# A layer of three mixers and product-key experts in one launch: a query projection from rows that are not yet normalised, another order of the mixers' outputs, and rotary tables made at the start

## The reference, cut to what matters

```python
h = rms_norm(x, norm1_g)                          # x: 256 tokens x 1024
ua, qb, kb, vb, qc, kc, vc, gc = split(h @ w_in)
ya = rms_unit(s5_mixer(ua, ...))                  # state space, gelu, y * sigmoid(y @ w_glu), 256 wide
yb = rms_unit(moba_mixer(qb, kb, vb, ...))        # causal attention here: 8 heads of 64, 512 wide
yc = retention_mixer(qc, kc, vc, gc, ...)         # 4 heads of 64, a norm per head, silu gate
x = x + (concat([ya, yb, yc]) * mix_out_g) @ w_out
h2 = rms_norm(x, norm2_g)                         # rms_norm(x, g) = x * rsqrt(mean(x*x) + eps) * g
q = (h2 @ w_q).reshape(t, 8, 2, 64)
sc = einsum('thcd,hcnd->thcn', q, sub_keys)       # scores, then top 16 of 128, twice, then of the pairs
out = x + sum_k gate_k * gelu(h2 . u_emb[e_k]) * v_emb[e_k]   # 16384 experts, 16 per head and token
```

## Time and profile before

| | us |
|---|---|
| median of 3 runs | 925.8 |
| lowest, highest | 925.78, 928.47 |
| the profiled execution | 925.64 |
| its span | 923.9 |
| TensorE busy | 910.5 |
| VectorE, ScalarE, POOL busy | 688.7, 539.8, 425.2 |

### The profile page before, as it was taken

How to read it: one execution, slowest core, us unless ns; L and a number is a source line. 1 busy time by engine, 2 the same in 40 slices (tenths; PEclk the granted TensorE clock), 3 DMA queues, 4 the chain that set the end, 5 groups by cost and what they waited for, 6 DMA issues and landing times.

```text
span 923.9 us, 20024 instructions
## 1 busy us (share of the span) xinstructions
PE 910.5 (99%) x5900; PEld 823.4 (89%) x5900; DVE 688.7 (75%) x1533; ACT 539.8 (58%) x1061; POOL 425.2 (46%) x340
## 2 busy tenths in 40 slices
PE   8999999999999999999999999999999999999998
PEld 7777879999999999999999999888888888888886
DVE  7989421079998027888888886888888888888886
ACT  7658655555555555555555555665656565656563
POOL 5764286788888877777777775000000000000000
PEclk9999999999999999999999999999999999999999
DMA  9644050456666666566555656777677777777773
GB/s 333 228 159 157 27 205 1 160 187 226 228 229 229 226 209 206 193 199 198 189 198 192 196 190 215 252 242 245 232 245 241 242 236 244 244 243 234 243 244 125
DMA packets 67756, 191.53 MB, mean 207 GB/s; under 512 B 6673, under 2 KB 8593, under 8 KB 67729
## 3 DMA queue, kind: packets, MB, share of 16 engines
q1 hardware_dynamic: 67728, 191.19, 61.5%
HBM read 173.86 MB, written 17.30 MB: 207 GB/s over the span
## 4 chain that ended last, share of the span: by engine, by line
PE 75%; POOL 11%; issue 7%; ACT 3%; DVE 2%; DMA 0%; POOLq 0%; SPq 0%; DVEq 0%
PE ps L429 23%; PE ps L431 22%; PE ps L430 22%; POOL w_lo L1600 11%; PE ps L717 3%; PE ps L414 1%; DVE ps L774 1%; ACT w_hi L1277 1%; DVE routing L774 1%; ACT routing L1343 0%; POOL w_lo L1585 0%; DMA xs<-in_x 0%; PE ps L603 0%; PE ps L406 0%; ACT L1265 0%
## 5 line engine op out<-in xcount | busy, mean ns | idle before, releaser
L1495 ACT ACTIVATE w_hi<-raw 128x512 fp32r<-128x512 f32 x512 | 308.3, 628 | 137.0 <-PE ps L431 134.8
L1600 POOL TENSOR_TENSOR w_lo<-raw,w_hi 128x512 fp32r<-128x512 f32 x256 | 327.1, 1299 | 81.1 <-ACT w_hi L1495 80.3
L429 PE MATMUL ps<-h_hi,w_hi 128*128 128x256 f32 x1088 | 308.6, 284 | 1.8 <-POOL w_lo L1600 1.1
L431 PE MATMUL ps<-h_hi,w_lo 128*128 128x256 f32 x1088 | 307.9, 283 | 0.0
L430 PE MATMUL ps<-h_lo,w_hi 128*128 128x256 f32 x1088 | 307.8, 283 | 0.0
L774 DVE TENSOR_TENSOR w_lo<-raw,w_hi 128x512 fp32r<-128x512 f32 x256 | 177.4, 693 | 56.1 <-ACT w_hi L1495 41.2
L429 PEld LDWEIGHTS ps<-h_hi,w_hi 128*128 128x128 f32 x1088 | 208.7, 192 | 2.7 <-POOL w_lo L1600 1.3
L430 PEld LDWEIGHTS ps<-h_lo,w_hi 128*128 128x128 f32 x1088 | 208.8, 192 | 0.0
L431 PEld LDWEIGHTS ps<-h_hi,w_lo 128*128 128x128 f32 x1088 | 208.8, 192 | 0.0
L429 PE MATMUL ps<-w_hi,hot_gate 128*128 128x512 f32 x512 | 199.2, 389 | 0.0
L430 PE MATMUL ps<-w_lo,hot_gate 128*128 128x512 f32 x512 | 199.2, 389 | 0.0
(11 more groups left out here) (207 smaller groups left out, 841.7 us busy)
## 6 DMA issues: line engine op xcount, KB each, us to landing
raw<-in_u_t SPq DMA_DIRECT2D x128, 512.0 KB, 3.4
raw<-in_v SPq DMA_DIRECT2D x128, 512.0 KB, 3.3
act_spill<-acts SPq DMA_DIRECT2D x62, 256.0 KB, 2.1
acts<-act_spill SPq DMA_DIRECT2D x62, 256.0 KB, 3.4
routing<-in_w_in SPq DMA_DIRECT2D x4, 2048.0 KB, 12.4
routing<-in_w_out SPq DMA_DIRECT2D x2, 2048.0 KB, 8.4
routing<-in_w_q SPq DMA_DIRECT2D x2, 2048.0 KB, 7.9
routing<-in_w_in SPq DMA_DIRECT2D x2, 1024.0 KB, 9.7
```

What stands on the lines that cost most here:

```text
L429: pe.matmul(dst, s_hi, m_hi, start=first and i == 0, stop=False)
L431: mm = pe.matmul(dst, s_lo, m_hi, start=False, stop=end)
L1495: A.activation(w_hi[:, 2 * (s % 2) + h, :], raw[:, s, h * HALF:(h + 1) * HALF], ACT.Copy)\
L1600: G.tensor_tensor(w_lo[:, slot, :], raw[:, s, h * HALF:(h + 1) * HALF], w_hi[:, slot, :].bitcast(F32), ALU.subtract).then_inc(lo_ready, 1)
```

## The change

It does four things.

1. Start: the rotary table is loaded ahead of x. `rope_q` and the key gains are made as soon as the state space constants are there, before the transposed x is scaled. The phase rates get a copy in PSUM (`phi_p`) for the second half of the turns; the second drive moves behind five slices of block two, and waits for these turns. ScalarE makes one slice more before the second sines and two more before the late exponentials; the second late scores follow the first at once.
2. Mixers: the state space product goes ahead of the last transposes of probabilities; the gelu, glu and gate follow between the two halves of the attention product; retention and state space outputs are transposed first, then 4 fillers and two output slices, then the attention's outputs.
3. Second norm: rows are transposed as they are after the residual sum, four blocks inside the second half of the output projection and four after the first query slice. The query projection works on them with the gain but without the root. Their high and low parts are written where the output projection's used parts stood (`H2_PLACE`). The key scores are multiplied by the root in ScalarE's copy.
4. Experts: VectorE keeps a full float32 copy with the gain (`rows_full`), TensorE spreads the roots over the partitions in PSUM by two products with the identity, VectorE multiplies, and ScalarE and VectorE split the results anew, each block in the place that a slice of the query projection has just left.

The diff, cut to its core:

```diff
@@ -56,9 +56,11 @@
 
 FRONT = 5 * KC
 TAIL = FRONT + 4 * KC
-MIX_ORDER = (2, 3, 4, 5, 6, 7, 0, 1)
-MIX_BANKS = (3, 4, 2, 7)
-OUT_BANKS = ((0, 1), (5, 6))
+MIX_ORDER = (6, 7, 0, 1, 2, 3, 4, 5)
+MIX_BANKS = (3, 7, 4, 5)
+OUT_BANKS = ((2, 6), (0, 1))
+ROW_BANKS = (2, 3, 0, 1)
+H2_PLACE = MIX_ORDER
 STATE_BANK = (6, 4, 4, 6)
...
+        phi_p = ps[:, 5, 0:8]
...
@@ -326,6 +332,7 @@
         def _(sp):
             sp.dma_start(vec[:], vecs).then_inc(params_in, 16)
             sp.dma_start(ident, consts[:, C_ID:C_ID + P]).then_inc(con_in, 16)
+            sp.dma_start(rawf[:, 256:256 + ROPE_N], rots[:, 0:ROPE_N]).then_inc(rope_in, 16)
             for t in range(TT):
                 sp.dma_start(xs[:, t, :], x[t * P:(t + 1) * P, :]).then_inc(x_in[t], 16)
             first = w_src[0].rearrange("(k p) n -> p k n", p=P)
@@ -336,7 +343,6 @@
...
-            sp.dma_start(rawf[:, 256:256 + ROPE_N], rots[:, 0:ROPE_N]).then_inc(rope_in, 16)
...
@@ -513,8 +519,10 @@
             pe.wait_ge(bT_ready, 1)
             drive(0)
             by_slices(1, range(2, KC))
+            by_slices(2, range(0, 5))
+            pe.wait_ge(turn_ready, S5_C)
             drive(1)
-            by_slices(2, range(KC))
+            by_slices(2, range(5, KC))
             turn_heads(0)
             by_slices(3, range(0, 6))
...
+            pe.wait_ge(ret_read, 1)
...
+                mm = pe.matmul(ps[:, 0, c], att0[:, g // 4, g % 4, :], mv[:, 0, c], start=True, stop=True)
+            mm.then_inc(o_psum, 1)
+
+            pe.wait_ge(y_ready, 1)
...
+            mm.then_inc(glu_psum, 1)
+
             pe.wait_ge(rp_ready, 1)
...
+            pe.wait_ge(ya_ready, 1)
...
+            mm.then_inc(yaT_psum, 1)
+
+            pe.wait_ge(pT_ready, 6)
...
+            mm.then_inc(o_psum, 1)
...
-            keep_warm(ident, 7, 10)
-            pe.wait_ge(moba_mix, 1)
-            transpose_mix(0)
...
-            keep_warm(ident, 4, 18)
-            for half_ in range(2):
-                pe.wait_ge(xn_ready, half_ + 1)
-                pe.wait_ge(xn1_ready, half_ + 1)
...
+            def turn_rows(ks):
+                for k in ks:
                     for t in range(TT):
-                        mm = pe.transpose(ps[:, k // 2, (k % 2) * S + t * P:(k % 2) * S + (t + 1) * P],
-                                          xn[:, t, k * P:(k + 1) * P], ident)
+                        mm = pe.transpose(ps[:, ROW_BANKS[k // 2], (k % 2) * S + t * P:(k % 2) * S + (t + 1) * P],
+                                          xs[:, t, k * P:(k + 1) * P], ident)
                     if k % 2:
                         mm.then_inc(t_psum, 1)
+
+            pe.wait_ge(ret_mix, 1)
+            transpose_mix(0)
+            pe.wait_ge(s5_mix, 1)
+            transpose_mix(1)
+            keep_warm(ident, 5, 4)
+            out_slices(0, range(0, 2))
+            pe.wait_ge(moba_mix, 1)
+            transpose_mix(2)
+            transpose_mix(3)
+            out_slices(0, range(2, KC))
+            out_slices(1, range(0, 3))
+            pe.wait_ge(sum2_ready, TT)
+            turn_rows(range(0, 4))
+            out_slices(1, range(3, KC))
+
             for n in range(2):
                 for k in range(KC):
                     if n == 0:
                         pe.wait_ge(th_ready, 2 * KC + k + 1)
                         pe.wait_ge(tl_ready, 2 * KC + k + 1)
+                    elif k == 0:
+                        pe.wait_ge(full2_ready, KC)
                     pe.wait_ge(lo_ready, FRONT + KC * (2 + n) + k + 1)
                     for h in range(4):
                         c = slice(h * P, (h + 1) * P)
                         mm = halves_product(ps[:, 4 * (1 - n) + h, 0:S],
-                                            [(w_hi[:, k % 4, c], w_lo[:, k % 4, c], h_hi[:, k, :], h_lo[:, k, :])],
+                                            [(w_hi[:, k % 4, c], w_lo[:, k % 4, c], h_hi[:, H2_PLACE[k], :], h_lo[:, H2_PLACE[k], :])],
                                             k == 0, k == KC - 1)
                     mm.then_inc(half_used, 1)
+                    if n == 0 and k == 0:
+                        pe.wait_ge(sum2_ready, 2 * TT)
+                        turn_rows(range(4, KC))
+                    if n == 1 and k == 2:
+                        pe.wait_ge(rows_ready, 1)
+                        pe.wait_ge(pq_ready, 4)
+                        for t in range(TT):
+                            mm = pe.matmul(ps[:, 4, t * P:(t + 1) * P], rstd_rows[:, t, :], ident, start=True, stop=True)
+                        mm.then_inc(spread_psum, 1)
 
             def key_scores(t):
 
...
+                        if first and s == 0:
+                            pe.wait_ge(th_ready, 3 * KC + 4 * h + 4)
+                            pe.wait_ge(tl_ready, 3 * KC + 4 * h + 4)
...
+            dve.wait_ge(rope_in, 16)
+            did(tt(cols(V_GQK + HD + ROPE, HD - ROPE), cols(V_GQK + HD + ROPE, HD - ROPE), cols(V_GQK + ROPE, HD - ROPE),
+                   ALU.mult))
+            half_rope = ROPE // 2
+            did(tt(rope_q[:, 0], rope[:, 0], cols(V_GQK, ROPE).unsqueeze(1).to_broadcast([P, TT, ROPE]), ALU.mult))
+            for a, b in ((0, half_rope), (half_rope, 0)):
+                did(tt(rope_q[:, 1, :, a:a + half_rope], rope[:, 1, :, a:a + half_rope],
+                       cols(V_GQK + b, half_rope).unsqueeze(1).to_broadcast([P, TT, half_rope]), ALU.mult))
+            settle()
...
+            dve.wait_ge(u_ready, 1)
+            did(V.tensor_copy(phi_p, phi))
...
+            def out_sums(t):
...
+            out_sums(0)
...
+            out_sums(1)
+            settle()
+            step(tt(sums[:, 0:16], sums[:, 0:16], hsum, ALU.mult))
+            tt(sums[:, 0:16], sums[:, 0:16], hsum, ALU.mult).then_inc(ms_ready, 1)
...
+            residual(0)
+            transposed_low(V_G2, 2, range(0, 4), ROW_BANKS, 0)
+            rows_full(range(0, 4))
+            residual(1)
             dve.wait_ge(sumsq_2, 4)
             tt(ss_x, ss_2[:, 0:2], ss_2[:, 2:4], ALU.add).then_inc(ms_ready, 1)
+            transposed_low(V_G2, 2, range(4, KC), ROW_BANKS, 4)
+            rows_full(range(4, KC))
             rstd_of(6, 0, TT, rstd[:, 0:TT]).then_inc(r2_ready, 1)
             dve.wait_ge(r2_ready, 1)
+            V.tensor_copy(rstd_rows, rstd[:, 0:TT].unsqueeze(2).to_broadcast([P, TT, P])).then_inc(rows_ready, 1)
+            dve.wait_ge(full2_ready, KC)
+            dve.wait_ge(spread_psum, 1)
+            for k in range(KC + 2):
+                if k >= 2:
+                    dve.wait_ge(th_ready, 3 * KC + k - 1)
+                    tt(h_lo[:, H2_PLACE[k - 2], :], ps[:, 5 + (k - 2) % 3, 0:S], h_hi[:, H2_PLACE[k - 2], :].bitcast(F32),
+                       ALU.subtract).then_inc(tl_ready, 1)
+                if k < KC:
+                    if k >= 3:
+                        dve.wait_ge(tl_ready, 3 * KC + k - 2)
+                    tt(ps[:, 5 + k % 3, 0:S], hT[:, k, :], ps[:, 4, 0:S], ALU.mult).then_inc(scaled_ready, 1)
...
+                    if n == 2:
+                        act.wait_ge(half_used, FRONT + KC + k + 1)
...
-            slices_high(range(12, 14))
+            slices_high(range(12, 15))
             phase_sines(1)
-            slices_high(range(14, 15))
+            slices_high(range(15, 16))
             phase_sizes(1)
-            slices_high(range(15, 16))
+            slices_high(range(16, 17))
...
-            slices_high(range(28, 31))
+            slices_high(range(28, 33))
             late_exps(0)
-            slices_high(range(31, 33))
+            slices_high(range(33, 34))
             late_exps(1)
-            slices_high(range(33, 34))
+            slices_high(range(34, 35))
             projected(3)
...
+            out_squares(0)
+            act.wait_ge(glu_psum, 1)
+            A.activation(gate_s, ps[:, 7, :], ACT.Tanh, scale=0.5).then_inc(gate_ready, 1)
+            A.activation(spare, quarter, ACT.Sqrt)
...
+            transposed_high(V_G2, 2, range(0, 4), ROW_BANKS, 0)
+            slices_high(range(FRONT + 14, FRONT + 16))
+            squares_2nd(0)
+            slices_high(range(FRONT + 16, FRONT + 20))
+            squares_2nd(1)
+            slices_high(range(FRONT + 20, FRONT + 21))
+            transposed_high(V_G2, 2, range(4, KC), ROW_BANKS, 4)
...
+            for k in range(KC):
+                if k < 4:
+                    slices_high(range(FRONT + 3 * KC + 4 + k, FRONT + 3 * KC + 5 + k))
+                act.wait_ge(scaled_ready, k + 1)
+                act.wait_ge(half_used, FRONT + 3 * KC + k + 1)
+                A.activation(h_hi[:, H2_PLACE[k], :], ps[:, 5 + k % 3, 0:S], ACT.Copy).then_inc(th_ready, 1)
...
+                             scale=rstd[:, t:t + 1]).then_inc(sc_ready, 1)
...
+            act.wait_ge(r2_ready, 1)
             high(0, 0, 0)
             queries(1)
             keys_turn(0, first=True)
```

(44 more changed lines are left out.)

178 lines of the change are left out of this document (54 added, 124 removed).

## The result

| | us |
|---|---|
| changed kernel, median of 5 runs | 921.8 (920.0 to 922.95) |
| kernel before, beside it, median of 5 | 926.5 (925.8 to 928.5) |
| ratio after : before, 95% interval | 0.9943 (0.9932 to 0.9953) |
| profiled execution of the changed kernel | 920.0, span 917.5 |

The change gains 0.57%, 4.7 us between the medians. The forecast was 919.4, its range 917.4 to 922.4: right in sign and within the range, 2.4 us too low, with one of the rivals on the measured value. The profiled execution was put at 919.2 and measured 920.0: its span, 917.5 us, is the sum's own (923.9 less 6.4), and the other 0.8 us lie around it (2.5 us, not 1.7).

A forecast was written before the change was run, and what follows sets the result against it. TensorE was taken as the bound, with all gains before the first expert tile. Terms of 13.45 us go and 7.07 come, a gain of 6.4: 925.64 to 919.2, by the median 919.4; range 917.4 to 922.4.

The forecast's parts named there:

- the raw rows: Second norm to hand-over: transposing unnormalised rows removes 4.1, 0.2 and 0.5 us, and brings 0.5 and 2.5 us.
- 0.5 us for fewer switches between narrow and wide multiplies: On TensorE: five fewer switches between narrow and wide multiplies gain 0.5 us in the sum.
- Waits ahead of slices 36 to 38: Before block five's end: TensorE waits 0.5, 1.1 and 0.1 us behind ScalarE's late queue, +1.7 us, bounds 0 and 3.
- mixer waits of 0.35, 0.15 and 0.5: Mixer outputs: TensorE waits 0.15 us for the state space part, 0.35 for VectorE's first low part, 0.5 for the attention.
- the 0.57 at the last projection: Before the first expert tile, kernel before: TensorE waits 0.57 us for the last projection.
- +0.47: Start: the rotary table's DMA ahead of x delays x and the loads behind it by 0.47 us, bounds 0.4 and 1.5.
- The rotary products: Front, VectorE: three small products fall from 3.79 to 0.5 us; copied phase rates cut a turns' product from 2.29 to 1.23.
- The fillers of 0.9: Mixer outputs: 8 recorded fillers on TensorE instead of 20, counted as 0.9 us that comes.
- The table loads: ScalarE, mixer outputs: three table loads become one; a load takes 1.28 us and the first activation follows without more.
- The gap: Hand-over to the experts: TensorE idles 2.5 us until POOL's first low part, where it is 0.5 now; bounds 0.5 and 3.8.
- rival C: TensorE's clock falls, with fewer fillers and a 2.5 us gap; about 2.1 us a fall; chance 0.09 once, 0.04 four times.
- C once: A single fall of TensorE's clock, costing about 2.1 us and giving 921.5 us; chance 0.09.

The follow-up runs named there:

- the kernel with the tile ahead: Against the changed kernel, ScalarE makes the first expert tile's first high part ahead of blocks 6 and 7 of the scaled rows' rounded copies; 918.8 us, ratio 0.9924.

## Why the prediction was right, and where it was not

**The chain.** By distance and by the prediction's terms, part 1 was put at 2.8 and measured 2.9; part 2 at 2.2, measured 2.55 (145.85 to 143.30); the raw rows at 1.8, measured 1.33 (143.30 to 141.97). The sum, 6.8, was met at 6.77: the last two errors cancel, which is luck. The 0.5 us for fewer switches between narrow and wide multiplies, a term of the prediction's sum, stands in no row, and no run tells it apart. By places: block five 86.6, measured 86.50; first output slice 107.5, 107.69; tile 159.4, 159.40.

**Waits ahead of slices 36 to 38** were put at 1.7 and measured 0.98 in two waits, behind POOL; mixer waits of 0.35, 0.15 and 0.5 measured 0.26 and 0.25, and the 0.57 at the last projection stayed.

**The start.** +0.47 matched to the hundredth (16.96 to 17.43), and that was luck. The issue of x did move by 0.46 (1.67 to 2.13), but the traces put the same row up to 3.3 us apart, and with the table behind x again it didn't come back.

**The rotary products** went from 3.79 us to 0.36, as reasoned. For the second turns' product (2.29 to 1.23) the size was right and the reason wrong, as shown above.

**The fillers of 0.9** were booked as a cost. They cover a wait of the same size, so taking them out gives nothing.

**The table loads.** The prediction read off that the first activation follows the load without more. Those rows can't show it: the exponential there waits 3.06 us for VectorE. The changed kernel's rows do:

```profile
67.05 1.28 ACT L1396 ACT_TABLE_LOAD   x1
68.34 0.60 ACT L1396 ACTIVATE routing<-routing,small 128x256 f32<-128x256 f32 x1
```

The load ahead of the exponentials starts at 67.05 us, lasts 1.28, and the first exponential follows at 68.34. The Trainium skill, "ScalarE: Activation LUTs", What ACT_TABLE_LOAD costs, counts 2.66 us with the drain; by this trace the drain isn't there, and the term of 1.28 stands.

**The gap** was put at 2.5, its end at POOL's first low part, and was 2.49.

**The step that failed** is the weighing of rival C. The prediction said, against a fall: clock full in all slices, with idle of 1.9 us among them. That was one execution. In the trace without the 18 fillers, where this piece of the program is the same, the clock does fall at that very place, and the mean clocks say that it most likely does in other executions of the kernel before; so the trace of before was weak evidence against a fall at a longer gap. In the six kernels that have the 2.49 us gap unfilled, 20 of 27 executions have a mean clock of 0.998 or less, and four of the six traces show the clock at 0.50 behind the gap; in the six with a shorter or filled gap it is 2 of 31. The mean clock is a rough sign: it counts a fall at the start and the clock behind the last product too. One of the 20, the traced execution without the mixers' fillers (0.997), has no fall behind the gap, but one at the start and a long end at 0.50.

The price was put at 2.1 and is 1.4 to 1.5 us behind this gap. It was taken from the opening (18 multiplies in 4.2 us); that stretch is longer than what a fall behind the gap slows, and the profile has no lower clock for it (its level was inferred from multiplies about twice as far apart as later ones). C once, 921.5 us, is what the median shows, and deserved most of the forecast's chance. That its figure fits to 0.3 us is luck, since a price that is too high makes up for what the next paragraph finds.

**The rest of the difference** lies around the span. It was taken from the kernel before as 1.7 us. That kernel has 1.7 to 1.85 in each of its 38 executions, the changed kernel 1.75 to 3.1, with a middle value of 2.5. So the median can be read as 917.5 (the span without a fall) and 1.5, 0.7 and 1.8: 921.5. That is an account of it, not proof: with the gap filled the median stayed at 921.4. What these 0.7 us are is open. They don't go with the clock: the kernel with the tile ahead has 2.5 to 2.8. They come in kernels with at most 5,864 recorded multiplies, the kernel before without fillers among them (up to 2.8), and in none with 5,874 or more; no run tells the reason.

## What to carry to other kernels

Before a gap is accepted in TensorE's program, look at what stands ahead of the weights' high part in ScalarE's order; a block moved by two places was worth 1.7 us of the chain here and 2.6 us by the median, more than the whole rearrangement of the norm. A clock that stays full behind an idle time in one trace says little: look at the mean clock of all executions, and price the fall in a trace that shows one. Compare variants by a distance within the trace that leaves the first loads out.

## What the runs showed of the hardware that was not expected

The granted clock fell to 0.50 for about 3 us behind 1.86 us of idle time (in one trace; in that of the kernel before it stayed full at the same place), behind 2.49 us in four of six traces, and behind 3.75 us in the one trace that has it. At the start it fell in the two traces that wait 1.91 and 2.38 us for w_in, and in none of those that wait less. Where a distance shows the cost it is 1.2 to 1.5 us. In the three kernels with 0.81 us at the hand-over, one of fourteen executions has a mean clock under 0.999.

A small VectorE operation with two SBUF inputs can be held up beside POOL far beyond its own length. In the changed kernel this sum of 256 numbers stands in the middle of six low parts of POOL and takes 1.07 us: it ends at 135.30, as POOL's fifth does (128.98 and five sixths of 7.57: 135.29). In the kernel before it took 0.21 us, beside the last 0.2 us of a low part.

```profile
128.98 7.57 POOL L1651 TENSOR_TENSOR w_lo<-routing,w_hi 128x512 fp32r<-128x512 f32 x6
...
134.23 1.07 DVE L796 TENSOR_TENSOR small<-small 128x2 f32<-128x2 f32 x1 [0.81 <-ACT routing L1521]
```
